# A split-precision decoder layer on one core: x's high part first, own banks for units 3 and 4, one weight split moved

## The chip, the core and the metric

The kernel runs on one core of one Trainium2 chip. The metric is the device time of one execution in microseconds, the median of the runs. The engines are called by short names: PE (TensorE, matrix products), DVE (VectorE), ACT (ScalarE), POOL (GpSimd) and SP (SyncE, here the queue that loads weights).

## The reference, cut to what matters

One layer of a decoder on 16 + 512 prompt positions and 8 sample tokens (536 columns in the kernel), width 1024, feed-forward width 2816:

```
x = x + 1/2 * (silu(n1(x) @ w_gate) * (n1(x) @ w_up)) @ w_down      # FFN 1
z = n2(x) @ w_in -> u (pool group) | q | k | v
x = x + concat(pool(u), window_attention(q, k, v)) @ w_out
x = x + 1/2 * (silu(n3(x) @ w_gate') * (n3(x) @ w_up')) @ w_down'   # FFN 2
n(x) = x * rsqrt(mean(x^2) + eps) * gain
```

`pool` is a trailing mean over 2, 4, 8 and 16 positions per channel group, minus the token, with a linear map per group. Attention has a window of 128, two key/value heads, eight query heads, normalised and rotated q and k, and a sink per head.

## The kernel before

**Data.** x lies transposed in `xT`: eight tiles (KD = 8) of 128 channels by 536 columns. Every product is made of three, so that it is nearly exact: a value is split in a high part (rounded to the PE's format) and a low part (the rest), and hi*hi + lo*hi + hi*lo are added up in PSUM. ACT makes the high parts (`split_hi` for a weight unit, L726; `x_hi` for a tile of x times the gain, L730), DVE the low ones (`split_lo`, L945; `x_lo`, L951).

**Units.** A weight unit is 128 output rows by eight tiles. PE works through it in `product` (L409): per tile, three pairs of operands on two halves of 268 columns, so 6 matmuls, 48 per unit. FFN 1 has 44 such units (0 = gate, 1 = up, 2 = gate, 3 = up, ...). Raw weights come through a ring of four slots `raw`, loaded by SP; whi and wlo have two slots each, so `split_hi(c)` waits until unit c - 2 is done (`unit_done`). The result of an even unit lies in PSUM pair 0, of an odd one in pair 1. Besides these there are the PSUM pairs `nsum` (norm sums and the spread norm) and `turn` (attention only).

**The norm** is applied after the product: DVE multiplies a unit's PSUM by `rstd` when it takes it out (`step_a`: gate L992, then silu on ACT L770, hid L997 and L1001, hhi on ACT L773, hlo L1005). `rstd` comes from the squares of x: POOL squares and adds tiles 0 to 3 (L1276 to L1282), ACT squares tiles 4 to 7 (L754), DVE adds those and POOL's sum (L972, L976), PE sums over the partitions with six small products (`norm_sums`, L427), ACT takes the root, DVE the reciprocal, PE spreads it over the partitions (`norm_spread`, L434), ACT copies it out (L742).

**Order at the start.** ACT: whi of unit 0 (behind the load of `fixed`, the constants and gains), eight tiles of xhi, whi of unit 1, four squares, whi of unit 2, root. DVE: wlo of unit 0, eight tiles of xlo, wlo of unit 1, the additions, wlo of unit 2. PE: unit 0, tile by tile, each behind its tile of xlo; unit 1 with the norm in it after five and six tiles; then a loop over the pairs of units from unit 2 on, in which a unit waits until the unit before the last has been taken out (`evacuated`).

**Attention.** Eight steps (i = 0 to 7), each with `turn_probs(i)` (PE transposes the probabilities, L604), `scores(i + 2)` (L592), `attend(i)` (L613), and one further piece of PE's work behind it: units of w_in, pool maps, `decode_attend` at i = 5. ACT copies probT (`out_probT`, L851), makes the high part of the result (`out_hi`, L857) and the exponentials (`exps`). DVE: `normalise(i + 1)` (L1129 to L1132), `maxima(i + 2)` (L1118 to L1123), `out_lo(i)` (L1140), and in between pool means (L1089), pool outputs (L1103) and weight splits. POOL's window sums (L1312) of pool group 3 and its `pool_lo` (mlo, L1344) wait for `normalise` at two places (`prob_ready` 6 and 7). At i = 6 PE begins unit 1 of w_out with `out_product(1, [0])` between `turn_probs(6)` and `attend(6)`; it waits for wlo of that unit (split 9), for seven `exps` and for three `pool_lo`. `turn_probs(7)` waits for `out_lo(6)` and `normalise(7)`. Everything is ordered by hand, by the order of the code for each engine and by semaphores.

## Time and profile before

| | |
|---|---|
| median of 3 runs | 965.12 us (965.09 to 965.76) |
| profiled run | 965.15 us |
| its span, first to last instruction | 963.4 us |
| PE busy | 943.8 us, 98% |
| DVE busy | 425.2 us, 44% |
| ACT busy | 274.0 us, 28% |
| POOL busy | 99.7 us, 10% |
| chain that ended last, by engine | PE 95%, DVE 3%, issue 1% |

All times below are microseconds from the start of the span, if not marked otherwise. Busy time tells only where work is; what an edit is worth is read from the waits of PE and from the chain that ended last. Adjacent operations of one engine overlap a little in the records, since each is recorded from its issue to its end; the distance from start to start is what one costs in a row.

### The profile page before, as it was taken

To read this page: it belongs to the slowest core of one execution; us is meant where nothing else is said; L and a number is where in the kernel's file an instruction comes from. 1 tells how busy PE (TensorE), PEld (TensorE's weight loads), DVE (VectorE), ACT (ScalarE), POOL (GpSimd) and SP (SyncE) were. 2 spreads that over 40 slices of the span, in tenths; PEclk is the share of its full clock that TensorE was granted. 3 is DMA by queue.
4 is the path that set the end of the run, shared out by engine and by line. 5 is a ranking of instruction groups with operands and counts; after the bars stand their busy time and mean duration, and the time that the engine had idled before them with its cause. 6 is when DMAs were issued, how large, how long until landed. Compare 5 with 4: busy or idle time off the path is not lost.

```text
span 963.4 us, 18000 instructions
## 1 busy us (share of the span) xinstructions
PE 943.8 (98%) x7556; PEld 920.8 (96%) x7556; DVE 425.2 (44%) x527; ACT 274.0 (28%) x382; POOL 99.7 (10%) x78
## 2 busy tenths in 40 slices
PE   5999999999999999999998999999999999999998
PEld 4999999999999999999865899999999999999998
DVE  7444444444443434343775575444444444322221
ACT  5322222222222122133455324223222232211110
POOL 4000000000002212133212451000000000000000
PEclk9999999999999999999999999999999999999999
DMA  6222222222332222152300122222223223333310
GB/s 236 88 87 87 87 87 87 90 90 89 108 108 91 90 90 73 45 178 83 111 23 22 57 87 89 96 100 87 87 88 102 93 87 103 120 106 107 112 41 22
DMA packets 24791, 87.57 MB, mean 91 GB/s; under 512 B 3232, under 2 KB 3616, under 8 KB 24768
## 3 DMA queue, kind: packets, MB, share of 16 engines
q1 hardware_dynamic: 23008, 84.45, 26.7%
q10 hardware_dynamic: 1760, 2.81, 0.8%
q8 instruction: 15, 0.25, 0.1%
q14 instruction: 8, 0.07, 0.0%
HBM read 83.31 MB, written 3.60 MB: 90 GB/s over the span
## 4 chain that ended last, share of the span: by engine, by line
PE 95%; DVE 3%; issue 1%; POOL 0%; DMA 0%; ACT 0%; POOLq 0%; DVEq 0%
PE ps L409 90%; PE ps L592 1%; PE ps L613 1%; DVE xlo L951 1%; PE ps L604 0%; DMA fixed<-fixed 0%; PE ps L427 0%; PE ps L589 0%; PE ps L515 0%; DVE wlo L945 0%; DVE small L1118 0%; POOL sqsum L1270 0%; PE ps L434 0%; PE ps L644 0%; PE ps L624 0%
## 5 line engine op out<-in xcount | busy, mean ns | idle before, releaser
L409 PE MATMUL ps<-xhi,whi 128*128 128x268 f32 (+1 forms) x1568 | 321.8, 286 | 11.0 <-DVE xlo L951 11.0
L726 ACT CAST whi<-raw 128x1024 fp32r<-128x1024 f32 (+1 forms) x138 | 155.3, 1125 | 618.5 <-PE ps L409 615.7
L409 PE MATMUL ps<-xlo,whi 128*128 128x268 f32 (+1 forms) x1568 | 319.0, 285 | 0.0
L409 PE MATMUL ps<-xhi,wlo 128*128 128x268 f32 (+1 forms) x1568 | 317.9, 284 | 0.0
L409 PEld LDWEIGHTS ps<-xhi,whi 128*128 128x128 f32 x1568 | 242.8, 189 | 15.3 <-issue 12.3
L945 DVE TENSOR_TENSOR wlo<-raw,whi 128x1024 fp32r<-128x1024 f32 (+1 forms) x138 | 194.1, 1406 | 127.6 <-ACT whi L726 127.6
L409 PEld LDWEIGHTS ps<-xhi,wlo 128*128 128x128 f32 x1568 | 243.5, 189 | 0.0
L409 PEld LDWEIGHTS ps<-xlo,whi 128*128 128x128 f32 x1568 | 243.4, 189 | 0.0
L409 PE MATMUL ps<-hhi,wlo 128*128 128x268 f32 (+1 forms) x704 | 143.0, 285 | 0.0
L409 PE MATMUL ps<-hlo,whi 128*128 128x268 f32 (+1 forms) x704 | 142.9, 284 | 0.0
L409 PE MATMUL ps<-hhi,whi 128*128 128x268 f32 (+1 forms) x704 | 142.6, 284 | 0.0
L409 PEld LDWEIGHTS ps<-hhi,whi 128*128 128x128 f32 x704 | 109.3, 188 | 0.0
L409 PEld LDWEIGHTS ps<-hhi,wlo 128*128 128x128 f32 x704 | 109.3, 188 | 0.0
L409 PEld LDWEIGHTS ps<-hlo,whi 128*128 128x128 f32 x704 | 109.0, 188 | 0.0
L992 DVE TENSOR_TENSOR gate<-ps,rstd 128x536 f32<-128x536 f32 (+1 forms) x44 | 31.2, 709 | 123.2 <-PE ps L409 119.7
L1001 DVE TENSOR_TENSOR hid<-ps,hid 128x536 f32<-128x536 f32 (+1 forms) x44 | 31.2, 708 | 121.7 <-PE ps L409 121.5
L1268 POOL TENSOR_TENSOR sq<-xT 128x536 f32 (+1 forms) x16 | 17.9, 1118 | 376.9 <-DVE xT L1026 357.1
L951 DVE SCALAR_TENSOR_TENSOR xlo<-xT,fixed,xhi (+1 forms) x24 | 40.1, 1693 | 0.0
L1270 POOL TENSOR_TENSOR sqsum<-sqsum,sq 128x536 f32<-128x536 f32 (+1 forms) x16 | 37.2, 2325 | 1.3
L997 DVE TENSOR_TENSOR hid<-act_gate,rstd 128x536 f32<-128x536 f32 (+1 forms) x44 | 30.9, 702 | 2.0 <-ACT act_gate L770 2.0
L1005 DVE TENSOR_TENSOR hlo<-hid,hhi 128x536 f32 (+3 forms) x44 | 30.9, 702 | 0.0
L409 PE MATMUL ps<-mhi,whi 128*128 128x260 f32 x128 | 26.1, 285 | 3.0 <-DVE wlo L945 2.6
(142 smaller groups left out, 486.8 us busy)
## 6 DMA issues: line engine op xcount, KB each, us to landing
raw<-gu SPq DMA_DIRECT2D x88, 512.0 KB, 3.3
raw<-d SPq DMA_DIRECT2D x32, 704.0 KB, 3.9
raw<-w_in SPq DMA_DIRECT2D x10, 512.0 KB, 3.6
raw<-w_out SPq DMA_DIRECT2D x8, 512.0 KB, 4.0
...
ckT<-ck SPq DMA_DIRECT2D x1, 512.0 KB, 5.1
cv<-cv SPq DMA_DIRECT2D x1, 512.0 KB, 5.7
```

The costliest lines, as they stand in the source:

```text
L409: last = nc.tensor.matmul(dst[:, s, 0:n], w[:, c % 2, kk, :], x[:, k, c0 + s * n:c0 + (s + 1) * n], start=(k == 0 and w is whi and x is hi ...
L592: last = nc.tensor.matmul(dst[j], qT[rows, j, t * P:(t + 1) * P], kT[rows, t * P:(t + 2) * P], start=False, stop=True, skip_group_check=True)
L613: last = nc.tensor.matmul(turn[rows, 0, :], tok[:, (t + b) * P + g * HD:(t + b) * P + (g + 1) * HD], probT[:, b, :], start=(b == 0), stop= ...
L726: nc.scalar.copy(whi[:, c % 2, 0:t, :], raw[:, c % RAW, 0:t, :]).then_inc(whi_ready, 1)
L945: nc.vector.tensor_tensor(wlo[:, c % 2, 0:t, :], raw[:, c % RAW, 0:t, :], whi[:, c % 2, 0:t, :].bitcast(F32), ALU.subtract).then_inc(wlo_r ...
L951: nc.vector.scalar_tensor_tensor(out=tile(xlo, d, it, c0, 2 * n, step), in0=tile(xT, d, it, c0, 2 * n, step), scalar=gain(g, d, it, step), ...
L992: nc.vector.tensor_tensor(halves(gate[:, cols], n), pair[0][:, :, 0:n], halves(rstd[:, cols], n), ALU.mult).then_inc(evacuated, 1)
L997: nc.vector.tensor_tensor(hid[:, cols], act_gate[:, cols], rstd[:, cols], ALU.mult).then_inc(silu_scaled, 1)
L1001: nc.vector.tensor_tensor(halves(hid[:, cols], n), pair[1][:, :, 0:n], halves(hid[:, cols], n), ALU.mult).then_inc(evacuated, 1)
L1005: nc.vector.tensor_tensor(tile(hlo, f, it, c0, 2 * n), hid[:, cols], tile(hhi, f, it, c0, 2 * n).bitcast(F32), ALU.subtract).then_inc(hlo_ ...
L1268: nc.gpsimd.tensor_tensor(sq[:, c0:c0 + 2 * n], x_d, x_d, ALU.mult).then_inc(sq_ready, 1)
L1270: nc.gpsimd.tensor_tensor(sqsum[:, c0:c0 + 2 * n], sqsum[:, c0:c0 + 2 * n], sq[:, c0:c0 + 2 * n], ALU.add).then_inc(sqsum_ready, 1)
```

## The change

**At the start.** ACT makes whi of unit 0 without waiting for `fixed`. DVE zeroes 256 columns of `hid` first, and PE makes four f32 products on them (`warm_up`, results unused). PE then works unit 0 in two passes (`early`): for each tile the products of xhi with whi and wlo, then for each tile those of xlo with whi. Unit 1 is in two passes as well, those with whi first. Unit 2 (the third) goes into the PSUM pair `turn`, with the norm's sums after tile 1 and its spreading after tile 3; unit 3 (the fourth) goes into `nsum` once rstd is copied out. The loop begins with unit 4. POOL's squares are gone: ACT squares all eight tiles, DVE adds them up in tile 0 of `sqx`. The splits of units 2 and 3 stand ahead of the norm on ACT and DVE, instead of behind it.

**In the attention.** Split 9, the second unit of w_out, moves on ACT from between `out_probT(5)` and `out_hi(5)` to the end of step 4, and on DVE from the end of step 5 to the end of step 4.

In the diff, cut to its core, the first block is PE's (WARM is 4), the next two are ACT's, the last three DVE's.

```
+        def warm_up():
+            pe.wait_ge(zeros_made, 1)
+            for _ in range(WARM):
+                nc.tensor.matmul(nsum[:, 0, 0:2 * P], hid[:, 0:P], hid[:, 0:2 * P], start=True, stop=True)
+        def early(c, dst, pairs, n, wait, first=False, last=False):
+            for k in range(KD):
+                for i, (w, x) in enumerate(pairs):
+                    wait(k, i)
+                    for h in range(2):
+                        done = nc.tensor.matmul(dst[:, h, 0:n], w[:, c % 2, k, :], x[:, k, h * n:(h + 1) * n],
+                                                start=(first and k == 0 and i == 0),
+                                                stop=(last and k == KD - 1 and i == len(pairs) - 1))
+            if last:
+                done.then_inc(unit_done, 1)
...
-                gate_or_up(0, None, wait_k=x_there)
-                gate_or_up(1, None, [0, 1, 2, 3, 4])
+                warm_up()
+                early(0, pair[0], [(whi, xhi), (wlo, xhi)], n, hi_there, first=True)
+                early(0, pair[0], [(whi, xlo)], n, lo_there, last=True)
+                early(1, pair[1], [(whi, xhi), (whi, xlo)], n, hi_1, first=True)
+                early(1, pair[1], [(wlo, xhi)], n, lo_1, last=True)
+                product(2, None, 2, turn, KD, xhi, xlo, 0, KD, c0, n, None, [0, 1])
                 norm_sums(0, c0, n)
-                gate_or_up(1, None, [5])
+                product(2, None, 2, turn, KD, xhi, xlo, 0, KD, c0, n, None, [2, 3])
                 norm_spread(0, c0, n, 1)
-                gate_or_up(1, None, [6, 7])
-            with pe.Fori(0, KF - 1) as it:
+                product(2, None, 2, turn, KD, xhi, xlo, 0, KD, c0, n, None, [4, 5, 6, 7])
+                pe.wait_ge(rstd_ready, 1)
+                product(3, None, 2, nsum, KD, xhi, xlo, 0, KD, c0, n)
+            f1 = 1 if second else 2
+            with pe.Fori(0, KF - f1) as it:
...
+        split_hi(0)
         act.wait_ge(fixed_loaded, 16)
-        split_hi(0)
...
-        for k in range(POOL_SQ, KD):
+        for k in range(KD):
             nc.scalar.activation(sqx[:, k, :], xT[:, k, :], ACT.Square).then_inc(sqx_ready, 1)
+            if k == 3:
+                split_hi(2)
         late_consts()
-        split_hi(2)
...
+        split_hi(3)
         norm(0, 0, NH_ALL)
...
             if i == 2:
                 split_next(8)
-            elif i == 5:
-                split_next(9)
             elif i == 6:
...
             elif i == 4:
                 pool_hi(2)
+                split_next(9)
...
+        for k in range(1, KD):
+            dve.wait_ge(sqx_ready, k + 1)
+            if k > 1:
+                dve.wait_ge(sqx_summed, k - 1)
+            nc.vector.tensor_tensor(sqx[:, 0, :], sqx[:, 0, :], sqx[:, k, :], ALU.add).then_inc(sqx_summed, 1)
+            if k == 4:
+                split_lo(2)
+        split_lo(3)
...
+                banks = [turn, nsum] if ua + f == 1 else pair
...
             elif i == 4:
                 pool_out(2)
-            elif i == 5:
                 split_next(9)
```

How the rows stand on the engines. PE, the beginning of unit 0, before (`[waits ...]` names the semaphores; a unit's first tile waits for the low parts of x and of the weight):

```order
L409 MATMUL ps<-xhi,whi 128x268 [waits xlo_ready,wlo_ready]
L409 MATMUL ps<-xhi,whi 128x268
L409 MATMUL ps<-xlo,whi 128x268 x2
L409 MATMUL ps<-xhi,wlo 128x268 x2
L409 MATMUL ps<-xhi,whi 128x268 [waits xlo_ready]
```

and in the changed kernel, whose lines have other numbers:

```order
L422 MATMUL ps<-hid 128x256 [waits zeros_made]
L422 MATMUL ps<-hid 128x256 x3
L430 MATMUL ps<-xhi,whi 128x268 [waits whi_ready,xhi_ready]
L430 MATMUL ps<-xhi,whi 128x268
L430 MATMUL ps<-xhi,wlo 128x268 [waits wlo_ready]
L430 MATMUL ps<-xhi,wlo 128x268
L430 MATMUL ps<-xhi,whi 128x268 [waits xhi_ready]
```

The products with xlo have moved from between the others to behind all eight tiles.

ACT behind the tiles of xhi, before:

```order
L726 CAST whi<-raw 128x1024 [waits raw_loaded1]
L754 ACTIVATE sqx<-xT 128x536 x4
L718 DMA maskf<-masks 128x512
L726 CAST whi<-raw 128x1024 [waits unit_done,raw_loaded2]
L758 ACT_TABLE_LOAD
```

and now:

```order
L769 CAST whi<-raw 128x1024 [waits raw_loaded1]
L797 ACTIVATE sqx<-xT 128x536 x4
L769 CAST whi<-raw 128x1024 [waits unit_done,raw_loaded2]
L797 ACTIVATE sqx<-xT 128x536 x4
L761 DMA maskf<-masks 128x512
L802 ACT_TABLE_LOAD
L802 ACTIVATE warm<-eps 128x1 [waits warmed]
L769 CAST whi<-raw 128x1024 [waits unit_done,raw_loaded3]
```

Four more squares stand ahead of the root, and whi of unit 3 as well.

DVE in attention steps 4 and 5, before, from behind the pool output of step 4 (`pool_out(2)`) on:

```order
L1129 TENSOR_TENSOR small<-small 128x4 [waits exp_ready]
L1130 RECIPROCAL small<-small 128x4 [waits step]
L1132 TENSOR_SCALAR prob<-prob,small 128x256 [waits step]
L1132 TENSOR_SCALAR prob<-prob,small 128x256 x3
L1140 TENSOR_TENSOR mlo<-ps,mhi 64x4x128 [waits ohi_ready]
L1225 COPY dout<-ps 64x32 [waits pair_filled]
L1225 COPY dout<-ps 64x32
L1118 TENSOR_REDUCE small<-ps 128x4 [waits scored]
L1120 TENSOR_TENSOR small<-small,qnrm 128x4 [waits step]
L1121 SCALAR_TENSOR_TENSOR small<-small,nsink 128x4 [waits step]
L1123 TENSOR_TENSOR small<-small,fixed 128x4 [waits step]
L945 TENSOR_TENSOR wlo<-raw,whi 128x1024 [waits whi_ready]
```

and now:

```order
L1149 TENSOR_SCALAR act_gate<-ps,fixed 128x520 [waits plo_ready,pair_filled]
L991 TENSOR_TENSOR wlo<-raw,whi 128x1024 [waits whi_ready]
L1175 TENSOR_TENSOR small<-small 128x4 [waits exp_ready]
L1176 RECIPROCAL small<-small 128x4 [waits step]
L1178 TENSOR_SCALAR prob<-prob,small 128x256 [waits step]
L1178 TENSOR_SCALAR prob<-prob,small 128x256 x3
L1186 TENSOR_TENSOR mlo<-ps,mhi 64x4x128 [waits ohi_ready]
```

The split stands ahead of `normalise(6)` now, not behind `maxima(7)`. SP's queue has the same rows in the same order.

## Rows read from the trace of the kernel before

**Rows 1.** Waits of PE, whole span (us in total, times, longest us).

```profile
PE ps L409 <- DVE xlo L951: 11.0, 4, 9.3
PE ps L409 <- DVE wlo L945: 2.6, 1, 2.6
PE ps L604 <- DVE mlo L1140: 1.8, 2, 1.4
```

**Rows 2.** Chain that ended last, from 0 to 70 us (start us, us, what).

```profile
4.95 1.05 ACT whi L726
...
7.66 9.84 DVE xlo L951 x6
...
20.06 3.96 PE ps L409 x30
...
28.29 41.83 PE ps L409 x336
```

**Rows 3.** Timeline of ACT, beginning (start us, us, engine, line, operation).

```profile
5.90 5.33 ACT L730 ACTIVATE xhi<-xT,fixed 128x536 fp32r<-128x536 f32 x8
11.71 1.05 ACT L726 CAST whi<-raw 128x1024 fp32r<-128x1024 f32 x1 [0.48 <-DMA raw<-gu]
...
12.66 2.27 ACT L754 ACTIVATE sqx<-xT 128x536 f32<-128x536 f32 x4
...
21.20 1.28 ACT L758 ACT_TABLE_LOAD   x1
```

**Rows 4.** Tile xhi to 20 us (ns min/median/max), then the timeline.

```profile
L951 DVE SCALAR_TENSOR_TENSOR xlo<-xT,fixed,xhi x8: 762/1589/1844, 7.6 to 18.1; 128x536 fp32r<-128x536 f32 x8
...
15.23 1.69 POOL L1282 TENSOR_TENSOR sqsum<-sqsum,sqx 128x536 f32<-128x536 f32 x1
...
19.93 2.35 DVE L972 TENSOR_TENSOR sqx<-sqx 128x536 f32<-128x536 f32 x3
```

**Rows 5.** DMA issues at 0.7 to 1.2 us; tile xT, eight loads.

```profile
raw<-gu SPq DMA_DIRECT2D x1, 512.0 KB, 4.0
...
DMA to landing us min/median/max: 4.2/5.2/5.9
```

**Rows 6.** Stretches: us, busy (count) of PE, PEld, DVE, ACT, POOL, PEclk, DMA, GB/s.

```profile
9.30:13.40 4.10, 4.08 (x16) 3.68 (x17) 4.10 (x3) 3.62 (x6) 4.02 (x3) 1.00 1.04 424
...
526.00:527.00 1.00, 1.00 (x2) 0.23 (x1) 0.93 (x5) 0.00 (x0) 0.00 (x0) 0.50 0.81 279
```

**Rows 7.** Timelines of ACT, DVE, POOL and PE, attention steps 4 to 7.

```profile
515.80 1.02 ACT L851 COPY probT<-ps 128x1024 f32<-128x1024 f32 x1
516.70 1.06 ACT L726 CAST whi<-raw 128x1024 fp32r<-128x1024 f32 x1
...
515.84 1.14 DVE L1132 TENSOR_SCALAR prob<-prob,small 128x256 f32<-128x256 f32 x4
...
521.59 1.23 DVE L1118 TENSOR_REDUCE small<-ps 128x4 f32<-128x1024 f32 x1
...
523.33 1.22 DVE L945 TENSOR_TENSOR wlo<-raw,whi 128x1024 fp32r<-128x1024 f32 x1
...
517.12 2.45 POOL L1312 TENSOR_TENSOR wsum<-wsum 128x528 f32<-128x528 f32 x2 [5.04 <-DVE prob L1132]
519.65 1.28 POOL L1344 TENSOR_TENSOR mlo<-act_gate,mhi 128x520 fp32r<-128x520 f32 x1
...
517.32 1.93 PE L613 MATMUL ps<-probT,tok 128*64 128x512 f32 x4
...
525.67 3.47 PE L613 MATMUL ps<-probT,tok 128*64 128x512 f32 x4
...
530.62 1.07 PE L604 MATMUL ps<-fixed,prob 128*128 128x128 f32 x8
```

**Rows 8.** Timeline of DVE, attention step 0, beside GpSimd's window sums.

```profile
483.29 1.03 DVE L1121 SCALAR_TENSOR_TENSOR small<-small,nsink 128x4 f32<-128x4 f32 x1
```

**Rows 9.** The page's costliest groups (busy us, mean ns).

```profile
L1001 DVE TENSOR_TENSOR hid<-ps,hid 128x536 f32<-128x536 f32 (+1 forms) x44 | 31.2, 708 | 121.7 <-PE ps L409 121.5
```

More of the change, by code:

```diff
@@ L95 @@
 NORM_AT = (1, 2, 5)
-POOL_SQ = 4
-SQSUM_AT = (POOL_SQ, POOL_SQ + KD, POOL_SQ + 2 * KD)
+SQSUM_AT = (0, KD, 2 * KD)
+WARM = 4
 def tiles_of(u):
@@ L455, in ffn_products, with hi_there, lo_there, hi_1 @@
             else:
-                gate_or_up(0, None, wait_k=x_there)
-                gate_or_up(1, None, [0, 1, 2, 3, 4])
+                def hi_there(k, i):
+                    if i == 0:
+                        pe.wait_ge(xhi_ready, k + 1)
+                    if k == 0:
+                        pe.wait_ge(wlo_ready if i else whi_ready, 1)
+                def lo_there(k, i):
+                    pe.wait_ge(xlo_ready, k + 1)
+                def hi_1(k, i):
+                    if k + i == 0:
+                        pe.wait_ge(whi_ready, 2)
+                def lo_1(k, i):
+                    if k == 0:
+                        pe.wait_ge(wlo_ready, 2)
+                warm_up()
[4 more added lines that the diff above has]
+                product(2, None, 2, turn, KD, xhi, xlo, 0, KD, c0, n, None, [0, 1])
                 norm_sums(0, c0, n)
-                gate_or_up(1, None, [5])
+                product(2, None, 2, turn, KD, xhi, xlo, 0, KD, c0, n, None, [2, 3])
                 norm_spread(0, c0, n, 1)
-                gate_or_up(1, None, [6, 7])
-            with pe.Fori(0, KF - 1) as it:
-                gate_or_up(0, it, f=1)
-                gate_or_up(1, it, f=1)
+                product(2, None, 2, turn, KD, xhi, xlo, 0, KD, c0, n, None, [4, 5, 6, 7])
[3 more added lines that the diff above has]
+            with pe.Fori(0, KF - f1) as it:
+                gate_or_up(0, it, f=f1)
+                gate_or_up(1, it, f=f1)
             def down(d, it):
@@ L966, in _ @@
         split_lo(1)
-        for i, k in enumerate(range(POOL_SQ + 1, KD)):
-            dve.wait_ge(sqx_ready, i + 2)
-            if i:
-                dve.wait_ge(sqx_summed, i)
-            nc.vector.tensor_tensor(sqx[:, POOL_SQ, :], sqx[:, POOL_SQ, :], sqx[:, k, :], ALU.add
-                                    ).then_inc(sqx_summed, 1)
-        dve.wait_ge(sqx_summed, KD - POOL_SQ - 1)
-        dve.wait_ge(sqsum_ready, POOL_SQ)
-        nc.vector.tensor_tensor(sqx[:, POOL_SQ, :], sqx[:, POOL_SQ, :], sqsum[:, :], ALU.add).then_inc(sqx_summed, 1)
-        split_lo(2)
+        for k in range(1, KD):
[6 more added lines that the diff above has]
+        split_lo(3)
         invert(1, nrm[:, 1, 0:BLKS], nrm[:, 0, 0:BLKS])
@@ L989, in step_a @@
             def step_a(f, it=None):
+                banks = [turn, nsum] if ua + f == 1 else pair
                 dve.wait_ge(unit_done, up_to(ua + 2 * f + 1, 4, it))
-                nc.vector.tensor_tensor(halves(gate[:, cols], n), pair[0][:, :, 0:n], halves(rstd[:, cols], n),
+                nc.vector.tensor_tensor(halves(gate[:, cols], n), banks[0][:, :, 0:n], halves(rstd[:, cols], n),
                                         ALU.mult).then_inc(evacuated, 1)
@@ L1000, in step_a @@
                 dve.wait_ge(silu_scaled, up_to(f0 + f + 1, 2, it))
-                nc.vector.tensor_tensor(halves(hid[:, cols], n), pair[1][:, :, 0:n], halves(hid[:, cols], n),
+                nc.vector.tensor_tensor(halves(hid[:, cols], n), banks[1][:, :, 0:n], halves(hid[:, cols], n),
                                         ALU.mult).then_inc(evacuated, 1)
-                split_lo(ua + 2 * f + 3, it)
+                if ua + f:
+                    split_lo(ua + 2 * f + 3, it)
                 dve.wait_ge(hhi_ready, up_to(f0 + f + 1, 2, it))
@@ L1268, in square @@
             nc.gpsimd.tensor_tensor(sq[:, c0:c0 + 2 * n], x_d, x_d, ALU.mult).then_inc(sq_ready, 1)
-            pool.wait_ge(sq_ready, up_to(SQSUM_AT[i - 1] + d, 1, it))
+            pool.wait_ge(sq_ready, up_to(SQSUM_AT[i - 1] + d + 1, 1, it))
             nc.gpsimd.tensor_tensor(sqsum[:, c0:c0 + 2 * n], sqsum[:, c0:c0 + 2 * n], sq[:, c0:c0 + 2 * n],
@@ L1272, in square @@
             pool.wait_ge(sqsum_ready, up_to(SQSUM_AT[i - 1] + d + 1, 1, it))
-        pool.wait_ge(x_loaded[0], 16)
-        nc.gpsimd.tensor_tensor(sqsum[:, :], xT[:, 0, :], xT[:, 0, :], ALU.mult).then_inc(sqsum_ready, 1)
-        for k in range(1, POOL_SQ):
-            pool.wait_ge(x_loaded[k], 16)
-            nc.gpsimd.tensor_tensor(sqx[:, k, :], xT[:, k, :], xT[:, k, :], ALU.mult).then_inc(sq_ready, 1)
-            pool.wait_ge(sq_ready, k)
-            pool.wait_ge(sqsum_ready, k)
-            nc.gpsimd.tensor_tensor(sqsum[:, :], sqsum[:, :], sqx[:, k, :], ALU.add).then_inc(sqsum_ready, 1)
         pool.wait_ge(nsum_filled, 1)
```

11 lines of the change are left out of this document (7 added, 4 removed).

## The prediction

> **What bounds the kernel now.** TensorE. The view of waits lists all idle time of TensorE (PE) that the profile puts down to somebody [rows 1]: 11.0 us behind the low parts of x (9.3 us of them before its first product), 2.6 us behind one split of a weight, 1.8 us behind the attention's low parts. The rest of the span PE computes, so an edit pays only where it takes away one of these gaps or what follows from it. The chain of waits at the start [rows 2] names the path: whi at 4.95, then wlo, then six low parts of x in 9.84 us, and only at 17.5 PE itself. From 28.29 on, 336 products take 41.83 us without a break, 0.1245 us each, so a unit of 48 costs 5.98 us. That point decides what the beginning is worth: units 0 and 1 are done at 28.25, unit 2 starts at 28.29, unit 4 would start at 28.29 + 2 x 5.98 = 40.25.
>
> **The beginning, part by part.**
>
> *GpSimd's squares removed.* The eight low parts of x take 11.28 us on DVE [rows 4]: median 1.59 us, smallest 0.76. The small one is the last, after GpSimd's last addition ended at 15.23 + 1.69 = 16.92 [rows 4]. The removed work is what slowed them. Alone I take 0.72 us each (three additions of the same size took 2.35, 0.78 each with their semaphore [rows 4]).
>
> *Start of PE.* The first weight unit lands 4.0 us after its issue at 0.74 [rows 5], at 4.74, not later than the 4.95 at which ACT started it behind the wait for `fixed`. So whi is there at 5.8, xhi of tile 0 at 5.7 + 0.67 = 6.4 (eight took 5.33, 0.67 each [rows 3]); tile 7 at 11.1, for x lands just ahead of it (4.2 to 5.9 us after each issue [rows 5]). DVE makes wlo by 5.8 + 1.22 = 7.0 (1.22 without GpSimd beside it, [rows 7]) and the low parts from 7.1 on, the last at 7.1 + 8 x 0.72 = 12.9. PE's first pass (4 products a tile, 0.50 us, against 0.67 for a tile of xhi) follows ACT: it ends at 11.1 + 0.5 = 11.65. The second pass has 16 products, 2.0 us, and finds xlo ahead of it (tile 6 is wanted at 13.15, there at 12.1). **Unit 0 ends at 13.65.**
>
> *Unit 1.* Its raw weights land at 11.71 [rows 3], whi at 12.8, wlo at 12.9 + 1.22 = 14.1: both ahead of need (13.65, 17.65). 5.98 us: end at 19.63.
>
> *Unit 2, in the banks `turn`, with the norm in it.* ACT squares all eight tiles now: 0.57 us each (2.27 for four [rows 3]), with whi of unit 2 between: 12.8 + 2.27 + 1.05 + 2.27 = 18.4. DVE's seven additions and wlo of unit 2 run behind: from 14.1, the fourth waits for square 4 (16.7), then wlo until 18.7, three more until 21.0. PE wants wlo at 19.63 and the sum at 19.63 + 1.5 = 21.1. No wait, but only 0.1 us of room: a slip here comes out at once. Norm products and spreading cost as before: unit 1 takes 28.29 - 20.06 = 8.2 with them [rows 2], 2.2 more than a unit alone. ACT needs its table for the root (1.28 us [rows 3]) and whi of unit 3 until 20.95, before the root at 22.4. Unit 2 ends at 19.63 + 5.98 + 2.2 = 27.8.
>
> *Unit 3, in the norm's banks `nsum`,* waits for rstd, copied out at about 25.4: no wait. It ends at 33.8. The cover for this is the chain behind rstd: ACT's table 1.28 [rows 3], seven operations of one x tile's size (gate and two products on DVE, silu and hhi on ACT, hlo and unit 2's gate on DVE) at about 0.71 each [rows 9], less what lies beside the table (the first gate), and wlo of unit 4 at 1.22 (its whi on ACT lies beside them): 1.28 + 6 x 0.71 + 1.22 = 6.8 us, until 32.2, against 33.8: 1.6 us of room. **Unit 4 starts at 33.8 instead of 40.25: 6.4 us gained.** The queues of SP are the same row for row; raw slots come free earlier.
>
> *The warm-up.* PE's products between 9.3 and 13.4 go at 16 in 4.10 us [rows 6], 0.255 each, half of the later pace, although that row's clock column stands at 1.00; afterwards they are at 0.1245. PE had stood idle before. The four f32 products on zeros can start at about 1.0. In the attention four records of 512 f32 columns, two products, take 3.47 us at half clock [rows 7]; four products of 256 columns are as many columns, so about 3.5 us: until 4.5. They block nothing, since PE has no operand before 6.4. If they raise the clock, the first pass costs what stands above; if it is low until 10, a tile of pass 1 takes 4 x 0.225 = 0.9 until then (0.255 less PE's waits), and pass 1 ends at 12.1 instead of 11.65, 0.5 us lost. If it is low until 13.4, as now, about 2.0 us are lost. I take 0: two passes that wait for ACT anyway hide most of it. Beginning: 6.4 us, between 4.4 and 6.9 (the high end: whi 0.2 earlier still, and no gap around the norm).
>
> **The split of w_out's unit 1 in attention step 4.** Now DVE reaches it at 523.33, behind the maxima of step 7 (521.59) [rows 7]; PE waits 2.6 us for it [rows 1] and then has another loss, which no wait shows: attend of step 6 takes 3.47 us where that of step 5 took 1.93 [rows 7], at a granted clock of 0.50, 1.2 GHz [rows 6], after the idle time. Together 2.6 + 1.55 = 4.2 us, but they don't all come back, since the split now stands ahead of other things. All times here are those of the trace before, without the shift from the beginning:
> - ACT: whi (1.06) goes ahead of probT of step 5, which moves from 515.80 to 516.85 and ends at 517.87; attend of step 5 starts then, not at 517.32 [rows 7]. Costs 0.55.
> - DVE: after pooling output 2 (ends 514.5) it waits for whi until 516.9, splits until 518.15, and only then normalises step 6: four products of 1.14 [rows 7] with two small steps ahead, 1.55 in all (515.43 to 516.98), now ready at 519.7. It was idle until 519.90 before, so out_lo(5) loses only the 0.55.
> - Behind normalise(6) stands GpSimd: window sums 2.45 and mlo 1.28 [rows 7] now run from 519.8 to 523.65, and out_product(1) waits for that mlo (`plo_ready`). So a wait of about 1.1 us (522.55 to 523.7) takes the place of 2.6.
> - attend(6) then runs 524.4 to 526.3 at full clock, and PE next wants the low part of step 6 for its turn of step 7, which started at 530.62 [rows 7]. DVE's way to that: maxima(7) from 522.1, 1.8 us, exponentials on ACT 2.4, normalise 1.55, out_lo 0.7: 528.55 and more.
> In that chain small DVE operations run beside GpSimd, and one of 4 columns took 1.03 us beside it instead of 0.16 [rows 8]. By that row one of the three can lose up to 0.87, which would leave 1.2 of gain. I add 0.35 and take the turn of step 7 at 528.9, **1.7 us earlier**, between 1.0 and 2.4 (no shift of attend, no contention). What follows, through mlo of pool group 3, moves with it.
>
> The Trainium skill (page "SBUF — State Buffer", section "Who interferes with whom") says that a VectorE instruction with two SBUF inputs contends with a GpSimd one that reads SBUF, and that whoever comes second is blocked until the other has ended. That speaks against this edit, which puts 3.7 us of GpSimd's work beside DVE's maxima. By it the first small operation after the reduction, due at 523.4, would wait until mlo has ended at 523.65, 0.25 us, and the gain would be 1.8. The rule speaks for the removed squares too, and there the trace agrees (0.76 against 1.59).
>
> **Sum.** 6.4 + 1.7 = 8.1 us. The profiled run has 965.15 us for a span of 963.4; its sum is 957.05, and the median before, 965.12, is 0.03 lower: 957.0.
>
> **The rivals.**
> 1. *The beginning is held up by more* (chance 0.13): the clock stays at 1.2 GHz until 13.4, or the sum of squares, with 0.1 us of room, is late. For: PE ran at half pace until 13.4 in this profile. Against: the warm-up gives it work before. It costs 1 to 2 us more: 958.0 to 959.0.
> 2. *The attention gives nothing* (0.08): the waits at 522.5 and before the turn of step 7 add up to 2.6 us near each other, the clock falls again, and with 0.55 + 1.55 the gain is gone: 958.7. Against: an idle stretch of 1.4 us [rows 1] came with no fall.
> 3. *More is gained* (0.06): attend is not delayed and the beginning reaches 6.9: 955.8 or less.
> 4. *Slower* (0.02), by one mechanism: the pairs of units in the first loop. Units 2 and 3 are emptied late (31 and 34.4), and if the chain gate, silu, product, split didn't keep up with 11.95 us a pair, each of the 20 iterations would repeat the wait. It decides from 8.1 / 20 = 0.41 us per iteration; at 0.6 the time is 957.0 + 12 = 969. Against: PE has no wait there [rows 1], and DVE's four operations and two splits of a pair take 4 x 0.71 + 2 x 1.22 = 5.3 us.
> 5. *The change doesn't do what it says* (0.01): xhi isn't ready before the low parts were, since x lands late, and only the attention gains: 963.4.
>
> **How the numbers follow.** Forecast as worked out: 0.70, 957.0. The range takes in rivals 1 to 3 and the bounds (6.9 + 2.4 = 9.3; 4.4 + 1.0 = 5.4, of which both ends together are unlikely): 955.3 to 959.2. 0.2%, about what a measurement of this kernel can tell from no change, is 1.9 us. Faster 0.97, same 0.01, slower 0.02.
>
> **What would show it.** After: first product on xhi near 6.4; low parts of x 0.7 us apart; unit 0 ends near 13.7, the norm products near 21.1; unit 4 starts near 33.8, or the chain behind rstd has no room. In the attention, no wait of PE for wlo but one of about 1 us for GpSimd's mlo, attend(6) at 1.93 us, no stretch at 0.50, and the turn of step 7 some 8.1 us before 530.62 (522.5). Wrong would be: PE cold in unit 0 up to its end, a wait for the squares over 0.5 us, a wait for rstd or evacuation before unit 3 or 4.

## The result, and the profile after

The changed kernel takes **957.50 us** (median of 4 runs, 957.28 to 957.74); the kernel before takes 965.44 in the same session (4 runs, 965.09 to 966.33). The ratio is 0.9916, with a 95% interval of 0.9899 to 0.9934: 7.9 us gained, where 8.1 were forecast. The profiled run took 957.28 us for a span of 955.5, against 963.4 before. The times of the kernel before fall into two groups: of its 38 executions during the experiments, the 13 with a mean granted clock of 0.998 took 964.89 to 965.21 us and the 25 with 0.996 took 965.57 to 966.78, so its median moves with how many of each fell into it. The profile of [rows 1] to [rows 9] is of the first kind (965.15), and that of the changed kernel is of its fastest execution (mean granted clock 1.00, the other three 0.998). From here on "the changed kernel" is the one of the diff; its lines have other numbers than those of the kernel before (product L410, `early` L430, `warm_up` L422, `split_hi` L769, `x_hi` L773, `split_lo` L991, `x_lo` L997, `turn_probs` L647, `attend` L656).

The page's first lines, busy time and the chain that ended last by engine:

```profile
PE 944.8 (99%) x7564; PEld 923.0 (97%) x7564; DVE 421.7 (44%) x531; ACT 276.4 (29%) x386; POOL 88.5 (9%) x71
...
PE 96%; issue 1%; DVE 1%; ACT 1%; POOL 1%; DMA 0%; POOLq 0%; DVEq 0%
```

PE's busy time is as before (944.8 against 943.8 us), the span is shorter: idle time went, not work. The view of PE's waits (us in total, times, longest) answers to [rows 1]:

```profile
PE ps L647 <- DVE mlo L1186: 2.4, 3, 1.4
...
PE ps L422 <- DVE hid L980: 1.2, 1, 1.2
PE ps L410 <- issue: 1.1, 1, 1.1
```

The 9.3 us before the first product have become 1.2 before the zeros and 1.5 between zeros and xhi (the timeline below). The wait for wlo, 2.6 us, is gone. In its place stand 1.1 us put down to "issue" (it is the wait for GpSimd's mlo, read below) and a third wait of `turn_probs`.

The chain of waits in the beginning (start us, us, what) answers to [rows 2]:

```profile
4.75 0.71 ACT whi L769
...
6.49 14.06 PE ps L430 x96
20.55 1.48 PE ps L410 x12
22.03 1.23 PE ps L446 x12
...
25.51 49.60 PE ps L410 x401
```

DVE is not in it any more; whi and one tile of xhi (5.70 to 6.45) stand ahead of PE. In [rows 2] PE's part of the chain starts behind the low parts.

PE's timeline in the beginning (start us, us, engine, line, operation):

```profile
1.20 3.78 PE L422 MATMUL ps<-hid 128*128 128x256 f32 x8 [1.20 <-DVE hid L980]
6.49 0.81 PE L430 MATMUL ps<-xhi,whi 128*128 128x268 f32 x2 [1.51 <-ACT xhi L773]
...
9.95 0.65 PE L430 MATMUL ps<-xhi,wlo 128*128 128x268 f32 x2
10.40 0.52 PE L430 MATMUL ps<-xhi,whi 128*128 128x268 f32 x2
10.75 0.41 PE L430 MATMUL ps<-xhi,wlo 128*128 128x268 f32 x2
...
12.49 2.15 PE L430 MATMUL ps<-xlo,whi 128*128 128x268 f32 x16
14.47 0.41 PE L430 MATMUL ps<-xhi,whi 128*128 128x268 f32 x2
...
20.39 0.41 PE L410 MATMUL ps<-xhi,whi 128*128 128x268 f32 x2
...
21.87 1.40 PE L446 MATMUL ps<-ones,sqx 128*128 128x1 f32 x12
...
28.31 0.41 PE L410 MATMUL ps<-xhi,whi 128*128 128x268 f32 x2
...
34.23 0.41 PE L410 MATMUL ps<-xhi,whi 128*128 128x268 f32 x2
```

A product is two records here. Up to 10.40 a pair of halves takes 0.45 us from start to start (9.95 to 10.40), from 10.75 on 0.25. The second pass over unit 0 starts at 12.49, unit 1 at 14.47, unit 2 at 20.39, the norm's sums at 21.87, unit 3 at 28.31, unit 4 at 34.23.

The tile view of the low parts, with the smallest, median and largest time in ns, answers to [rows 4]; below it DVE's and ACT's timelines:

```profile
L997 DVE SCALAR_TENSOR_TENSOR xlo<-xT,fixed,xhi x8: 769/771/772, 7.0 to 11.9; 128x536 fp32r<-128x536 f32 x8
...
7.04 5.58 DVE L997 SCALAR_TENSOR_TENSOR xlo<-xT,fixed,xhi 128x536 fp32r<-128x536 f32 x8
...
18.23 2.35 DVE L1018 TENSOR_TENSOR sqx<-sqx 128x536 f32<-128x536 f32 x3
...
34.44 0.72 DVE L1046 TENSOR_TENSOR hid<-ps,hid 128x536 f32<-128x536 f32 x1 [0.94 <-PE ps L410]
...
25.54 0.61 ACT L785 COPY rstd<-ps 128x536 f32<-128x536 f32 x1 [1.98 <-PE ps L453]
```

All eight low parts take 0.77 us each; from start to start they are 0.69 apart, (5.58 - 0.77) / 7. The last additions of squares start at 18.23 and end at 20.58, 1.3 us ahead of PE. Unit 3 is taken out at 34.44. In the kernel before the same step stood here (its DVE timeline):

```profile
40.45 0.72 DVE L1001 TENSOR_TENSOR hid<-ps,hid 128x536 f32<-128x536 f32 x1 [2.95 <-PE ps L409]
```

So the beginning gained 40.45 - 34.44 = **6.0 us**.

In the attention, the timelines of PE, DVE and GpSimd answer to [rows 7]:

```profile
511.86 1.93 PE L656 MATMUL ps<-probT,tok 128*64 128x512 f32 x4 [0.42 <-ACT probT L897]
...
517.68 0.47 PE L410 MATMUL ps<-mhi,whi 128*128 128x260 f32 x2 [1.07 <-issue]
...
518.55 1.93 PE L656 MATMUL ps<-probT,tok 128*64 128x512 f32 x4
...
522.75 1.07 PE L647 MATMUL ps<-fixed,prob 128*128 128x128 f32 x8 [0.65 <-DVE mlo L1186]
...
517.39 0.20 DVE L1166 TENSOR_TENSOR small<-small,qnrm 128x4 f32<-128x4 f32 x1
...
516.30 1.28 POOL L1380 TENSOR_TENSOR mlo<-act_gate,mhi 128x520 fp32r<-128x520 f32 x1
```

`turn_probs(7)` starts at 522.75, before at 530.62 [rows 7], 7.87 us earlier: 6.0 from the beginning and 1.9 from here. `attend(6)` takes 1.93 us, where [rows 7] have 3.47. PE's wait at 517.68 ends 0.1 us after GpSimd's mlo (516.30 + 1.28 = 517.58), which is how the "issue" of the view of waits is to be read.

DVE's small operation at 517.39 ends at 517.59, right behind the same mlo. In the kernel before, this operation of GpSimd stood beside the one of [rows 8], which ran from 483.29 to 484.32:

```profile
483.24 1.07 POOL L1312 TENSOR_TENSOR wsum<-wsum 128x528 f32<-128x528 f32 x1
```

It ends at 484.31. Both small operations end 0.01 to 0.02 us after GpSimd's, though one took 0.20 us and the other 1.03.

### The profile page after: what moved, and what is told of

It is laid out like the page before. It is cut to its first block, busy times and chain, and to the rows that moved or that the text cites. A ratio compares the mean times of both kernels' runs of the same rounds, so it can differ in the third digit from the quotient of the medians.

```text
span 955.5 us, 18010 instructions
## 1 busy us (share of the span) xinstructions
PE 944.8 (99%) x7564; PEld 923.0 (97%) x7564; DVE 421.7 (44%) x531; ACT 276.4 (29%) x386; POOL 88.5 (9%) x71
## 4 chain that ended last, share of the span: by engine, by line
PE 96%; issue 1%; DVE 1%; ACT 1%; POOL 1%; DMA 0%; POOLq 0%; DVEq 0%
PE ps L410 90%; PE ps L430 1%; PE ps L635 1%; PE ps L656 1%; PE ps L647 0%; PE ps L446 0%; DMA raw<-gu 0%; PE ps L558 0%; PE ps L632 0%; ACT prob L885 0%; POOL sqsum L1315 0%; PE ps L453 0%; PE ps L687 0%; ACT whi L769 0%; PE ps L667 0%
## 5 line engine op out<-in xcount | busy, mean ns | idle before, releaser
L769 ACT CAST whi<-raw 128x1024 fp32r<-128x1024 f32 (+1 forms) x138 | 155.3, 1126 | 608.9 <-PE ps L410 605.3
L410 PE MATMUL ps<-xhi,whi 128*128 128x268 f32 (+1 forms) x1536 | 313.7, 285 | 0.0
L410 PE MATMUL ps<-xlo,whi 128*128 128x268 f32 (+1 forms) x1536 | 312.0, 285 | 0.0
L410 PE MATMUL ps<-xhi,wlo 128*128 128x268 f32 (+1 forms) x1536 | 311.1, 284 | 0.0
L991 DVE TENSOR_TENSOR wlo<-raw,whi 128x1024 fp32r<-128x1024 f32 (+1 forms) x138 | 194.2, 1407 | 133.3 <-ACT whi L769 133.3
L410 PEld LDWEIGHTS ps<-xhi,whi 128*128 128x128 f32 x1536 | 237.3, 188 | 2.8 <-issue 2.8
L410 PEld LDWEIGHTS ps<-xhi,wlo 128*128 128x128 f32 x1536 | 238.0, 188 | 0.0
L410 PEld LDWEIGHTS ps<-xlo,whi 128*128 128x128 f32 x1536 | 237.7, 188 | 0.0
L410 PE MATMUL ps<-hhi,wlo 128*128 128x268 f32 (+1 forms) x704 | 143.1, 285 | 0.0
L410 PE MATMUL ps<-hlo,whi 128*128 128x268 f32 (+1 forms) x704 | 143.0, 284 | 0.0
L410 PE MATMUL ps<-hhi,whi 128*128 128x268 f32 (+1 forms) x704 | 142.6, 284 | 0.0
L410 PEld LDWEIGHTS ps<-hhi,whi 128*128 128x128 f32 x704 | 109.3, 188 | 0.0
L410 PEld LDWEIGHTS ps<-hhi,wlo 128*128 128x128 f32 x704 | 109.3, 189 | 0.0
L410 PEld LDWEIGHTS ps<-hlo,whi 128*128 128x128 f32 x704 | 109.0, 188 | 0.0
L997 DVE SCALAR_TENSOR_TENSOR xlo<-xT,fixed,xhi (+1 forms) x24 | 34.4, 1460 | 0.0
L815 ACT ACTIVATE act_gate<-gate 128x536 f32<-128x536 f32 (+1 forms) x44 | 28.1, 638 | 0.5 <-DVE gate L1037 0.5
```

What stands on the lines that cost most here:

```text
L410: last = nc.tensor.matmul(dst[:, s, 0:n], w[:, c % 2, kk, :], x[:, k, c0 + s * n:c0 + (s + 1) * n], start=(k == 0 and w is whi and x is hi ...
L769: nc.scalar.copy(whi[:, c % 2, 0:t, :], raw[:, c % RAW, 0:t, :]).then_inc(whi_ready, 1)
L815: nc.scalar.activation(act_gate[:, cols], gate[:, cols], ACT.Silu).then_inc(silu_ready, 1)
L991: nc.vector.tensor_tensor(wlo[:, c % 2, 0:t, :], raw[:, c % RAW, 0:t, :], whi[:, c % 2, 0:t, :].bitcast(F32), ALU.subtract).then_inc(wlo_r ...
L997: nc.vector.scalar_tensor_tensor(out=tile(xlo, d, it, c0, 2 * n, step), in0=tile(xT, d, it, c0, 2 * n, step), scalar=gain(g, d, it, step), ...
```

## The experiments

Each kernel is the changed one with one edit, if not said otherwise. All ratios are against the kernel before as it ran in the same session. Its medians there, 965.73 to 966.08, lie 0.3 to 0.6 us above that of the result, because more of its executions had the mean granted clock of 0.996; so small steps are read from the traces. e5 and e9 do extra work whose results are not used.

### e1: the beginning alone

```
         # ACT, DVE: step 4
-                split_next(9)
         # ACT, DVE: step 5
+                split_next(9)
```

> The changed kernel with split 9 back in its old places (step 5 on ACT and DVE); only the beginning is changed. Theory (the beginning gives 5.9 us, the moved split 1.9): PE's 2.6 us wait for wlo before out_product(1) is back, attend(6) takes 3.4 us instead of 1.9 at a clock of 0.50, and the time is 957.5 + 1.9 = 959.4. Rival (the clock's fall hangs on the moment, not on the idle time): the wait is back but attend(6) stays at 1.9 us, and the turn of step 7 comes only some 0.4 us later than in the changed kernel: 957.9.

Measured: 959.27 us (959.22 to 959.59), ratio 0.9935 [0.9922, 0.9948]. PE's timeline in the attention, then a window of it (columns as in [rows 6]):

```profile
518.78 0.48 PE L410 MATMUL ps<-mhi,whi 128*128 128x260 f32 x2 [2.63 <-DVE wlo L992]
...
519.66 3.61 PE L656 MATMUL ps<-probT,tok 128*64 128x512 f32 x4
...
520.00:521.00 1.00, 1.00 (x2) 0.23 (x1) 0.93 (x5) 0.00 (x0) 0.00 (x0) 0.50 0.67 229
```

Both parts of the loss are back as [rows 1] and [rows 7] have them: the wait for wlo, 2.63 us, and the `attend` that follows it at 3.61 us and a granted clock of 0.50 (1.2 GHz). The moved split is worth 959.27 - 957.50 = 1.8 us beside the new beginning. The beginning alone is worth 5.8 us against the executions of the kernel before at 0.998 (some 965.1), as the 6.0 of the trace has it; the 6.5 against the session's median are more only through those at 0.996.

The trace of e1 shows something of the beginning too. PE's timeline and a window there:

```profile
7.53 0.52 PE L430 MATMUL ps<-xhi,whi 128*128 128x268 f32 x2
7.84 0.65 PE L430 MATMUL ps<-xhi,wlo 128*128 128x268 f32 x2
...
7.80:11.20 3.40, 3.40 (x18) 3.40 (x17) 3.40 (x6) 3.40 (x6) 0.00 (x0) 0.52 1.05 419
```

Here the first products on xhi, up to 7.8, went at the full pace (0.31 us from 7.53 to 7.84), then came a fall: 0.45 a pair and a granted clock of 0.52 until 11.2. In between PE had stood idle for 1.9 us, from the zeros to the first tile of xhi. So in this execution four products on zeros raised the clock (the shortest of their eight records takes 0.38 us, the median 0.63), and 1.1 us after PE had gone back to work it fell again. In the profile of the changed kernel all eight records on zeros take 0.63 us or more, and the products on xhi are at half pace from the first one (0.81 us for two records): there it had not risen by the end of the zeros. The two come out alike, at full pace from 10.4 in the one and from 11.0 in the other.

### e2: the attention alone

The kernel before, with split 9 moved on ACT and DVE as the diff has it, and nothing else.

> The kernel before with split 9 at the end of attention step 4; the beginning as before. Theory: the turn of step 7 comes 1.9 us earlier, at 528.7 instead of 530.6, and the time is 965.4 - 1.9 = 963.5. Rival (the two parts need each other): no gain here, 965.4.

Measured: 963.25 us, ratio 0.9976 [0.9967, 0.9986], 2.5 less than the session's median of the kernel before, but 1.85 less than its executions at 0.998 (some 965.1), where 1.9 was expected. Seven of nine executions lay between 963.21 and 963.29, with a mean granted clock of 1.00, two at 963.92 and 964.09, with 0.998; one more, at 1874.11, stands apart and is not used. The profile is of the one at 964.09, and there PE's timeline and a window show:

```profile
523.63 0.61 PE L409 MATMUL ps<-mhi,whi 128*128 128x260 f32 x2 [1.07 <-issue]
...
525.04 3.00 PE L613 MATMUL ps<-probT,tok 128*64 128x512 f32 x4
...
524.00:525.00 1.00, 1.00 (x6) 0.81 (x4) 0.97 (x4) 1.00 (x4) 0.00 (x0) 0.50 0.07 16
```

Around a wait of only 1.07 us, behind decode's sixteen products of 8 columns and the turn of step 6, the granted clock fell to 0.50 in this execution: `attend(6)` took 3.00 us instead of 1.93. In the profile of the changed kernel the same work and the same wait came with no fall. So the part of the gain that comes from the clock isn't had in every execution; where it is missing, 0.8 us are lost (964.09 - 963.25).

### e3: no products on zeros, and e4: six

```
-WARM = 4
+WARM = 0
```

is e3, which doesn't wait for the zeros either; e4 has `WARM = 6`.

> The changed kernel without the four products on zeros. Theory (they ended at 4.98, 1.5 us before the first product on x, and the clock rose at 10.4 all the same): they bought little; PE is slow until between 9.9 and 10.5, unit 0 ends at 14.4 as with them, 957.5 to 957.8. Rival (they brought the rise forward): PE is slow for up to two or three us longer, unit 0 ends at 15 to 16 and the time is 958.2 to 959.0.

> Six products on zeros instead of four. At half clock they last until 1.2 + 6 x 0.945 = 6.9, over the first operand's arrival at 6.45. Theory (the idle time between 4.98 and 6.49 is what kept the clock low): the clock rises by 8 at the latest, the first pass follows ACT and ends at 11.8 instead of 12.5, unit 0 at 13.75: 957.5 - 0.7 = 956.8. Rival (products on zeros don't count for the clock): rise at about 10.4 again, the first pass begins 0.4 later and ends 0.2 later: 957.7.

Measured: e3 957.45 us (957.01 to 957.72), ratio 0.9915 [0.9903, 0.9928]; e4 956.99 (956.68 to 958.94), ratio 0.9917 [0.9904, 0.9929]. PE's timeline in e4:

```profile
1.20 5.49 PE L422 MATMUL ps<-hid 128*128 128x256 f32 x12 [1.20 <-DVE hid L980]
...
7.07 0.51 PE L430 MATMUL ps<-xhi,wlo 128*128 128x268 f32 x2
7.42 0.41 PE L430 MATMUL ps<-xhi,whi 128*128 128x268 f32 x2
...
12.19 2.02 PE L430 MATMUL ps<-xlo,whi 128*128 128x268 f32 x15
```

In e3 the products on xhi begin at 6.47 and run at half pace until 10.8. With four products it is until 10.4: the warm-up of the diff is worth nothing that can be measured. Six, which last until 6.7, reach the first tile of xhi; from 7.07 on a pair takes 0.25 to 0.35 us (7.07 to 7.42). The zeros themselves ran at half pace to the last (0.63 us a record), so in this execution it took all of them; in that of e8 the same six end at 5.95, since the clock rose during them, and it stayed up over the 0.66 us until the first operand. Yet the first pass ends at 12.19, only 0.3 us before that of the changed kernel, for now it follows ACT's tiles, 0.69 apart, one of which had to wait 0.3 us for its load. Of the clock's loss at the beginning a longer warm-up returns 0.3 us by the trace. The 0.5 between the medians is less sure: the five executions of e4 reach from 956.68 to 958.94, and the two slowest have a mean granted clock of 0.997 and 0.996 instead of 1.00.

### e5: GpSimd's squares and additions back, with no use

```
+        for k in range(4):
+            pool.wait_ge(x_loaded[k], 16)
+            nc.gpsimd.tensor_tensor(sq[:, :], xT[:, k, :], xT[:, k, :], ALU.mult)
+            nc.gpsimd.tensor_tensor(sqsum[:, :], sq[:, :], sq[:, :], ALU.add)
```

Semaphores are left out; the addition is made from k = 1 on, for k = 0 a fill of two columns stands in its place. DVE waits for these eight steps behind its last split, so that they stand as early as they did.

> The changed kernel with GpSimd busy at the start again: four squares and three additions of one tile of x's size into buffers whose contents nobody uses (ACT and DVE still make the sum that is used). Theory (GpSimd's work is what slowed DVE's low parts): xlo takes some 1.5 us again instead of 0.70, is complete at 18 to 19 instead of 12.6, the second pass of unit 0 ends behind it, and the time is 957.5 + 4.5 = 962, between 961 and 963. Rival (DVE was slow for another reason, the loads landing in SBUF at the time): xlo stays at 0.70, 957.5.

Measured: 963.28 us (962.07 to 964.74), ratio 0.9972 [0.996, 0.9983]. The tile view and the chain:

```profile
L998 DVE SCALAR_TENSOR_TENSOR xlo<-xT,fixed,xhi x8: 764/1589/1590, 8.5 to 17.4; 128x536 fp32r<-128x536 f32 x8
...
8.60 9.63 DVE xlo L998 x8
...
24.73 1.48 PE ps L411 x12
```

The median low part takes 1.59 us again, to the hundredth that of [rows 4], and the last, after GpSimd is done at 16.3, 0.76. Eight of them are 9.63 us of chain, and unit 2 reaches its place at 24.73 instead of 20.55: 4.2 us, all of it from work whose result nobody uses. This shows the cause that the prediction had only read from one small row. The way of it can be read too: GpSimd's square of tile 2 runs from 10.29 to 11.72, and the low part that DVE begins at 10.71 ends at 12.30, 0.57 to 0.58 us after it; in the kernel before the low part from 15.65 to 17.49 ends 0.57 behind GpSimd's 16.92 [rows 4] as well. The two take turns. The Trainium skill's rule (page "SBUF — State Buffer", section "Who interferes with whom") that a VectorE instruction with two SBUF inputs contends with a GpSimd one that reads SBUF agrees with the pair 1.59 and 0.76. What is left of the difference in the profiled run (962.07 against 957.28) lies in the attention, where the clock fell once more after a wait of 1.06 us. The other executions reach up to 964.74, and the slower ones have the lower mean granted clock (0.998 up to 962.29, 0.996 at 963.3, 0.995 at 963.81 and 964.74); where their further slow stretches lie no trace shows.

### e6: the products of units 0 and 1 in the old order

```
-                early(0, pair[0], [(whi, xhi), (wlo, xhi)], n, hi_there, first=True)
-                early(0, pair[0], [(whi, xlo)], n, lo_there, last=True)
-                early(1, pair[1], [(whi, xhi), (whi, xlo)], n, hi_1, first=True)
-                early(1, pair[1], [(wlo, xhi)], n, lo_1, last=True)
+                product(0, None, 2, pair[0], KD, xhi, xlo, 0, KD, c0, n, x_there)
+                product(1, None, 2, pair[1], KD, xhi, xlo, 0, KD, c0, n)
```

> The changed kernel with units 0 and 1 in the old order of products (tile by tile behind its low part); everything else as changed. Theory (with GpSimd quiet the low parts come every 0.70 us, faster than a tile's six products of 0.745): PE starts at 7.8 instead of 6.5 and unit 0 ends at 15.0 instead of 14.4: 958.1. Rival (taking the high part first carries the gain): 960 or more.

Measured: 959.1 us (958.31 to 959.27), ratio 0.9927 [0.991, 0.9943]. Two windows:

```profile
8.00:13.20 5.20, 5.19 (x23) 5.20 (x24) 5.15 (x8) 4.72 (x8) 0.00 (x0) 1.00 1.04 419
13.20:18.20 5.00, 5.00 (x42) 5.00 (x41) 2.81 (x4) 3.20 (x7) 0.00 (x0) 1.00 0.68 224
```

PE starts at 8.01 instead of 6.49, the norm's sums at 23.98 instead of 22.03 (by the chains of both). With PE busy throughout, 23 records in 5.2 us stand against 42 in 5.0: the slow stretch moves with the start, from 10.4 to 13.2, and is somewhat longer. High parts first are worth 1.6 us by the medians and 1.95 by the traces: 1.5 of it is the earlier start.

### e7: DVE's split between `normalise(6)` and `out_lo(5)`

```
         # DVE, step 4
-                split_next(9)
         # DVE, step 5
+                split_next(9)
                 out_lo(i)
```

ACT's split stands where the kernel before has it.

> The changed kernel with split 9 at another place: on ACT in step 5, between out_probT(5) and out_hi(5), as before; on DVE in step 5 between normalise(6) and out_lo(5), where DVE was idle for 2.9 us before. Theory (the place in step 4 costs attend(5) 0.4 to 0.55 us and holds GpSimd and so out_product(1) up for 1.1): both waits are gone and the turn of step 7 comes 0.6 us earlier than in the changed kernel: 956.9. Rival (the turn of step 7 hangs on DVE's maxima(7) and ACT's exponentials, which don't move): 957.4.

Measured: 956.91 us (956.69 to 957.74), ratio 0.9909 [0.9892, 0.9926], 0.6 less than the changed kernel. PE waits neither for probT at step 5 nor for mlo before `out_product(1)`, but `turn_probs(7)`, at 522.21, waits 1.48 us for the low part of step 6. Of the 1.5 us that the two waits had cost, 0.5 come through; the rest becomes a new wait of 0.33 us for probT before `attend(6)` and 0.83 more before `turn_probs(7)`, which hangs on the chain maxima, exponentials, normalise, `out_lo`.

### e8: e7 and e4 together

> The split at the place of e7 and six products on zeros as in e4. Theory (independent parts): 957.5 - 0.6 - 0.5 = 956.4. Rival (one hides the other): as the better of the two alone, 956.9.

Measured: 956.38 us (956.18 to 956.44), ratio 0.9900 [0.9884, 0.9917]: 1.1 us less than the changed kernel, 0.6 + 0.5. Both gains add up, since they lie 500 us apart.

### e9: e1 with PE kept busy while it waits

```
             elif i == 6:
+                pe.wait_ge(exp_ready, 2 * QT - 1)
+                for _ in range(10):
+                    nc.tensor.matmul(pair[1][:, 0, 0:P], ident[:, :], ident[:, :], start=True, stop=True)
                 out_product(1, [0])
```

The results of the ten products are not used.

> As e1 (split 9 in its old places, so that PE has to wait for wlo before out_product(1)), with ten unused products of 128 f32 columns put ahead of out_product(1) on PE, some 2.3 us of work inside the 2.6 us of waiting. Theory (PE's idle time is what lets the clock fall): out_product(1) starts when it did, but attend(6) takes 1.9 us instead of 3.6 and the time is 959.3 - 1.6 = 957.7. Rival (the clock falls there for another reason): attend(6) stays at 3.4 to 3.6 and the time at 959.3 or, with products that last longer than the wait, above.

Measured: 957.52 us (957.13 to 958.45), ratio 0.9917 [0.9903, 0.993]. PE's timeline and a window:

```profile
516.14 2.40 PE L725 MATMUL ps<-fixed 128*128 128x128 f32 x20
518.93 0.48 PE L410 MATMUL ps<-mhi,whi 128*128 128x260 f32 x2 [0.40 <-DVE wlo L995]
...
519.82 1.93 PE L656 MATMUL ps<-probT,tok 128*64 128x512 f32 x4
...
520.00:521.00 1.00, 1.00 (x3) 0.28 (x3) 0.90 (x5) 0.07 (x1) 0.00 (x0) 1.00 0.75 188
```

`out_product(1)` starts at 518.93, not earlier than in e1 (518.78), yet the kernel is 1.75 us faster: `attend(6)` takes 1.93 us at 1.00 instead of 3.61 at 0.50. Of the loss in e1, 2.63 + 1.68 = 4.3 us, 1.7 is clock alone, and ten products of 128 columns in the idle time take it away, though their results are of no use. By this e1 with ten useless products is as fast as the moved split of the diff (957.52 and 957.50).

### e10: units 2 and 3 in the old banks

```
+                norm_sums(0, c0, n)
+                norm_spread(0, c0, n, 1)
+                pe.wait_ge(evacuated, 1)
+                product(2, None, 2, pair[0], KD, xhi, xlo, 0, KD, c0, n)
+                pe.wait_ge(evacuated, 2)
+                product(3, None, 2, pair[1], KD, xhi, xlo, 0, KD, c0, n)
...
-                banks = [turn, nsum] if ua + f == 1 else pair
+                banks = pair
```

These lines stand for those of the diff that put unit 2 in `turn`, with the norm in it, and unit 3 in `nsum`.

> The changed kernel with units 2 and 3 in PSUM pairs 0 and 1, as before: since these hold units 0 and 1 until rstd is there, the norm stands between units 1 and 2 and unit 2 waits for the first evacuation, unit 3 for the second. Theory (the own banks hide the chain sums, root, reciprocal, spread, rstd, gate behind PE's work): unit 2 starts at 25.5, unit 4 at 37.4 instead of 34.3: 957.5 + 3.1 = 960.6. Rival (the banks matter little, the gain is GpSimd's): below 958.5.

Measured: 962.56 us (961.75 to 963.94), ratio 0.9968 [0.9957, 0.9978]. The expectation missed by 2 us. One wait and two windows:

```profile
PE ps L410 <- DVE gate L1036: 1.4, 1, 1.4
...
25.70:29.30 3.60, 3.55 (x16) 3.55 (x17) 1.55 (x3) 1.84 (x3) 0.00 (x0) 0.50 0.00 0
29.30:33.00 3.70, 3.70 (x30) 3.70 (x30) 0.60 (x1) 0.00 (x0) 0.00 (x0) 0.96 0.00 0
```

The waits are 0.7 us for the sum of squares, 0.6 around the root and 1.4 for rstd and the first gate, 2.7 together. What the expectation left out is their consequence. They stand close together, with only the norm's small products between, and the granted clock falls: from 22.5 to 29.3 it is 0.50 to 0.54, 16 records in 3.6 us against 30 in 3.7. That is 1.8 us for the products until 29.3, and 0.9 for the spreading (1.55 us instead of the 0.66 after). 2.7 + 1.8 + 0.9 = 5.4, measured 962.56 - 957.50 = 5.1. In the trace unit 3 is taken out at 39.65 instead of 34.44, 5.2 us later, so the count comes out a little high. The unit between the norm and its users is what hides both. The edit undoes two things at once, the own banks and the norm's place inside a unit; old banks with the norm inside unit 1, as in the kernel before, were not run.

### e11: e8 with the maxima of step 7 ahead of decode's copy

```
             # DVE, step 5
                 out_lo(i)
+                maxima(i + 2)
                 dve.wait_ge(pair_filled, filled["so"])
```

> The kernel of e8 with maxima(7) ahead of the copy of dout on DVE in step 5. Theory (the turn of step 7 hangs on maxima(7), ACT's exponentials and normalise(7)): ACT can begin the exponentials right behind probT(6), 0.4 us earlier, and the time is 956.4 - 0.4 = 956.0. Rival (the turn hangs on attend(6) and out_hi): 956.4.

Measured: **955.73 us** (955.64 to 956.08), ratio 0.9899 [0.9883, 0.9914], the fastest of all: 10.0 us less than the kernel before, 1.8 less than the changed one. ACT's exponentials start right behind probT, at 516.26, and PE's timeline has

```profile
521.13 1.07 PE L647 MATMUL ps<-fixed,prob 128*128 128x128 f32 x8 [1.15 <-DVE mlo L1187]
```

The wait before `turn_probs(7)` is 1.15 us instead of 1.46 in e8: the chain that e7 had laid bare has lost one copy and the wait for it. That is 0.3 us, of 0.4 expected. The rest of the 0.65 between the medians is not shown to be the edit's: in the profiled executions PE is 0.45 us ahead already at the end of the first pass (11.71 against 12.16), which the edit does not touch; ACT's tiles of xhi came faster there (0.66 apart against 0.70).

## Why the prediction was right, and one term of it wrong

The forecast was 957.0 (955.3 to 959.2), measured 957.50. Point by point:

- **GpSimd's squares.** 0.72 us from one to the next were taken, 0.69 measured (0.77 for the operation itself), so the last ended at 12.62 for 12.9; e5 shows that they were the cause. The right row was the small one of eight.
- **Start of PE.** 6.4 forecast, 6.49 measured. First term of the sum right.
- **The warm-up, "I take 0": the term that was mis-sized.** Unit 0 was to end at 13.65 and ended at 14.47, 0.8 us late. Unit 2 kept that distance (20.39 for 19.63); unit 4, at 34.23 for 33.8, was 0.4 late, since the norm cost less and a unit took 5.92 us instead of 5.98. The text had 0.5 as the cost if the clock were low until 10; it was low until 10.4. Two things were overlooked: four products on zeros end at 4.98, and between them and the first operand at 6.5 PE is idle (e1's rows show a rise lost again behind that gap, the changed kernel's none at all); and a low clock costs more than ACT's lead hides, since pass 1 ran 0.9 us per tile against ACT's 0.69. e3 settles that the warm-up bought nothing, e4 that even a long enough one buys 0.3 to 0.5.
- **Sum of squares.** 0.1 us of room was forecast, 1.3 measured, and 0.8 of that is only PE's lateness. The rest is ACT and DVE being ahead of the sum by 0.4.
- **Norm and banks.** The norm costs 2.0 us over a unit (28.31 - 20.39 = 7.92, less 5.92), 2.2 forecast. rstd is copied at 25.54, for 25.4. wlo of unit 4 ends at 32.86 by DVE's timeline, 1.4 ahead of PE's 34.23, for 1.6. e10 shows what the banks and the norm's place hide: 5.1 us.
- **Beginning in all.** 6.4 forecast, 6.0 measured, inside 4.4 to 6.9. With 0.4 too much here and 0.2 too little in the attention, the total (7.87 us between the two profiled runs, 8.1 forecast) is closer than its terms; that much of it is luck.
- **The moved split.** `attend(5)` delayed by 0.42 (0.55 forecast); PE's wait before `out_product(1)` 1.07 (1.1); `attend(6)` at full clock; 1.9 gained against 1.7. The added 0.35 for small DVE operations beside GpSimd was not needed: the one that started at 517.39, with GpSimd's mlo running until 517.58, took 0.20 us, where [rows 8] have 1.03. It did wait, though, as did the one of [rows 8]: both ended with GpSimd's operation, as read above, so the price is what GpSimd has left to do, 1.0 us there and 0.2 here, of which 0.16 pass anyway. This agrees with the Trainium skill's rule (page "SBUF — State Buffer", section "Who interferes with whom") that whoever comes second is blocked until the other has ended. By it the prediction had 1.8 us of gain; here only 0.04 us of waiting came out of it.
- **Rival 1** (clock low until 13.4) came about in a smaller form, 0.8 us instead of 1 to 2. **Rival 2** (clock falls in the attention as well) wasn't in the profile after, but e2 shows it in the same code: two of nine executions by their times and clocks, one of them traced, at a price of 0.8. Its chance of 0.08 was low for a single execution; the median it didn't move. **Rival 4** (the loop) did not come: PE has no wait for a bank from unit 4 on, its chain runs from 25.51 for 49.6 us without a break. Nor did rivals 3 and 5.

The parts undone one by one come to more than the whole: 4.2 us of chain (e5), 1.6 (e6) and 5.1 (e10) against 6.0. They aren't independent. Each hides a part of what the others would expose: without own banks PE's early start ends in the wait for rstd; with slow low parts PE starts as early (6.47 in e5), but unit 0 then waits for them and ends at 18.63 instead of 14.47.

What stays open: why the clock falls around a wait of 1.07 us in one execution and not in another, and the scatter of e5. The length of the wait alone doesn't decide: the fall came 0.7 us after its end in the kernel before (at 525.4), 0.9 in e1 (519.7), 0.2 in e2 (523.8), and in e5 0.6 us after its beginning (521.5), read from windows of 0.25 us. e9 shows only that work in the idle time kept the clock up in the profiled execution.
